# Two output projections that begin inside the last head of their layer

## The chip, the cores and the metric

The kernel runs on one core of one Trainium2 chip. The metric is the device time of one execution in microseconds (us), the median of several runs. TensorE (PE in the rows) multiplies, ScalarE (ACT), VectorE (DVE) and GpSimd (POOL) work on whole tiles, SyncE (SP) issues the loads of the weights.

## The reference

A network of three layers over 512 tokens of width 1024, all in fp32. The change touches the mixers of the first two:

```
# layer 0, MLA: 8 heads of attention, causal softmax
p = softmax(mask(q_h @ k_h^T * scale));  o_h = p @ v_h          # for each head h
m = concat(o_0 .. o_7) @ mla_w_o                                # 1024 x 1024
h = h + rms_norm(m);  h = h + rms_norm(relu(rms_norm(h) @ w1)^2 @ w2)

# layer 1, HGRN2: 8 heads of gated linear recurrence in chunks of 32 tokens
o_h = intra-chunk part (masked k_rel x q_rel) + q_dec @ state   # state chained over 16 chunks
y_h = rms_norm(o_h) * silu(gate_h)
m = concat(y_0 .. y_7) @ hgrn_w_o                               # 1024 x 1024
h = h + rms_norm(m);  then the second MLP
# layer 2: three other mixers and an MLP, not touched
```

Both projections sum over the heads: head k contributes the k-th block of 128 rows of the weight. So a projection can start with the heads that are done, and needs the last head only for its last term.

## The kernel before

The five engines have programs of their own, written out by hand, that meet only through semaphores. Each engine works through its program in order.

**Weights.** All weights are a list of blocks of 128 x 1024 (512 KB). SP loads block b into slot b % 4 of `ring` (L249) when block b - 4 has been used, or, for most blocks, has been split. The right-hand operand is split in the same way (`a_hi`, `a_lo`), and `split_matmul` issues three matmuls for each k, hi x hi, hi x lo and lo x hi (L336 to L338), each 128x128 by 128x512. A tile of output is 8 values of k, thus 24 matmuls, into one PSUM bank. `ring_hi` and `ring_lo` have 4 slots too.

**A projection** of 8 tiles is `gemm_split_pe`: tile u goes to bank u % 4 after its bank is free (`mla_o_free`, `hgrn_o_free`) and its block is split. `to_m_act` squares and copies each finished tile (L561, L562) and then rounds the block four ahead. `to_m_dve` adds up the squares (L574) and then computes that block's rest. Behind the last tile `norm_pe` computes the norm.

**Last heads, MLA.** `mla_pe` goes through the heads. In turn h it projects head h + 1 (`head`, banks 0 to 2), transposes the probabilities of head h (`att_turn_pe`, L516, banks 3 to 5), computes the scores of head h + 1 (L470, banks 0 to 2), and multiplies head h's probabilities by its values (`att_out_pe`, L531, bank 6). ACT takes the exponentials (L491), copies the turned probabilities (`att_turned_act`, L523) and head h's output as `a_hi` (L818). DVE masks the scores (L480), divides (L499 the reciprocal, L506) and computes the low half `a_lo` (`low_y`, L899), which counts `mla_y`. In turn 7 there is no next head. `mla_o` begins behind it.

**Last heads, HGRN.** `hgrn_pe` runs `head(i, nxt, prev)`: the projections of head i + 1 (`project`, 24 matmuls each for q, f, v and g in banks 0 to 3), the norm of head i - 1 (`total`, L417, `spread`, L425, bank 7), and head i itself: pairs (L1314, bank 4), turned keys (L1319, bank 5), chunk states (L1288, banks 5 and 6), output (L1345 and L1350, bank 4). DVE chains the states (L1505), and when the norm is spread computes y and its two halves, which counts `hg_y_split`. ACT writes the turned keys to `kz` (L1416). Heads 1 to 6 are a loop. `head(7, False, True)` has no projections to issue. Behind it come `total(7)`, `spread(7)` and `hgrn_o`. The first four blocks of `hgrn_o` are rounded and split in turn 6, as the next head's blocks would be.

Of the kernel before, what the change touches and what calls it, by code (L numbers as in the profile page):

```python
# [17 lines left out]
NT = D // P  # L18
# [287 lines left out]
def gemm_pe(pe, M, name, tiles, per_tile, rhs, unroll, banks=4, looped=True, first_wait=None):  # L306

    used, free = M.sem("blocks_used"), M.sem(f"{name}_free")

    def tile(i, u):
        pe.wait_ge(free, u + 1 if i is None else i * unroll + (u + 1))
        for blk in range(per_tile):
            b = FIRST[name] + u * per_tile + blk
            wait_block(pe, M, b, i, unroll * per_tile)
            for k in range(BLK):
                kk = blk * BLK + k
                if first_wait and u == 0:
                    first_wait(kk)
                mm = pe.matmul(M.bank(u % banks), block_tile(M, b, k), rhs(kk),  # L320
                               start=(kk == 0), stop=(kk == per_tile * BLK - 1))
            mm.then_inc(used, 1)

    if looped:
        with pe.Fori(0, tiles // unroll) as i:
            for u in range(unroll):
                tile(i, u)
    else:
        for u in range(tiles):
            tile(None, u)  # L330

def split_matmul(pe, M, out, b, k, hi, lo, start, stop):
# [352 lines left out]
def mla_pe(pe, M, R):  # L686
    def total(name, n):
        pe.wait_ge(M.sem("norm_summed"), n + M.past(name, "summed"))
        norm_total_pe(pe, M, M.norm_bank(name), M.ssum).then_inc(M.sem("norm_total"), 1)

    def first_total():
        pe.wait_ge(M.sem("inputs_in"), 16)
        total("norm_0", NT)

    mla_in_pe(pe, M, {(2, 4): first_total, (3, 4): lambda: norm_root_pe(pe, M, "norm_0"),
                      (5, 2): lambda: total("q_lora", 4), (6, 0): lambda: norm_root_pe(pe, M, "q_lora")})

    pe.wait_ge(M.sem("norm_scaled"), 4 + M.past("q_lora", "scaled"))
    pe.wait_ge(M.sem("mla_in_free"), 6)
    for pair in range(4):  # L700
        b, at = FIRST["mla_rope"] + pair // 2, 4 * (pair % 2)
        if pair % 2 == 0:
            wait_block(pe, M, b)
        for k in range(4):
            mm = pe.matmul(M.bank(ROPE_BANK[pair]), block_tile(M, b, at + k), R.proj[:, k, :],
                           start=(k == 0), stop=(k == 3))
        mm.then_inc(M.sem("blocks_used" if pair % 2 else "rope_pairs"), 1)
        if pair == 0:
            total("kv_lora", 2)
        if pair == 1:  # L710
            norm_root_pe(pe, M, "kv_lora")
    pe.wait_ge(M.sem("norm_scaled"), 2 + M.past("kv_lora", "scaled"))

    pe.wait_ge(M.sem("mla_in_free"), 7)

    def head(h):
        b = FIRST["mla_heads"] + h
        wait_block(pe, M, b)
        for k in range(4):
            pe.matmul(M.bank(0), block_tile(M, b, k), R.proj[:, k, :], start=(k == 0), stop=(k == 3))  # L720
        for k in range(2):
            pe.matmul(M.bank(1), block_tile(M, b, 4 + k), R.proj[:, 4 + k, :], start=(k == 0), stop=(k == 1))
        if h == 0:
            pe.wait_ge(M.sem("rope_read"), 2)
        for t in range(QT):
            for k in range(2):
                mm = pe.matmul(M.bank(2)[:, t * P:(t + 1) * P], R.proj[:, 4 + k, t * P:(t + 1) * P],
                               block_tile(M, b, 6 + k), start=(k == 0), stop=(k == 1))
        mm.then_inc(M.sem("blocks_used"), 1)

    def scores(h):
        pe.wait_ge(M.sem("mla_heads_free"), h + 1)
        if h == 0:
            pe.wait_ge(M.sem("rope_turned"), 5)
        half = slice(0, P)
        att_scores_pe(pe, M, "mla", [(R.q[:, h % 2, :], R.k[:, h % 2, :]),
                                     (R.qr[half, h // 2, :], R.krz[:, h % 2, :])])

    head(0)
    scores(0)  # L740
    for h in range(MLA_H):
        if h + 1 < MLA_H:

            pe.wait_ge(M.sem("mla_masked"), h + 1)
            head(h + 1)
        att_turn_pe(pe, M, "mla", R.att, h, 0)
        if h + 1 < MLA_H:
            scores(h + 1)
        if h:
            pe.wait_ge(M.sem("mla_y"), h)  # L750
        att_out_pe(pe, M, "mla", R.att, h, 0, lambda k: R.v[:, h % 2, k * P:(k + 1) * P], 6)
    gemm_split_pe(pe, M, "mla_o", NT, 1, lambda k: M.a_hi[:, k, :], lambda k: M.a_lo[:, k, :], 4,
                  first_wait=lambda k: pe.wait_ge(M.sem("mla_y"), k + 1))
    norm_pe(pe, M, "mla_o", NT + 2)

def mla_act(act, M, R):
# [53 lines left out]
    for h in range(MLA_H):  # L811
        if h + 1 < MLA_H:
            head(h + 1)
        att_turned_act(act, M, "mla", R.att, h, 0)
        if h + 1 < MLA_H:
            att_exp_act(act, M, "mla", R.att, h + 1, 0)
        act.wait_ge(M.sem("mla_out"), h + 1)
        act.activation(M.a_hi[:, h, :], M.bank(6), ACT.Copy).then_inc(M.sem("mla_y_high"), 1)  # L818
        for j in MLA_O_AT.get(h, ()):
            round_block(act, M, FIRST["mla_o"] + j, fresh=True)  # L820
    to_m_act(act, M, "mla_o", 1, 4, 4, round_ahead(act, M))

MLA_O_AT = {5: (0,), 6: (1,), 7: (2, 3)}

def mla_dve(dve, M, R):
# [72 lines left out]

    att_mask_dve(dve, M, "mla", R.att, 0, 0, mask, MLA_SCALE)
    for h in range(MLA_H):
        if h:
            low_y(h - 1)
        att_divide_dve(dve, M, "mla", R.att, h, 0)
        if h + 1 < MLA_H:
            att_mask_dve(dve, M, "mla", R.att, h + 1, 0, mask, MLA_SCALE)
        for j in MLA_O_AT.get(h, ()):
            rest(FIRST["mla_o"] + j)  # L910
# [348 lines left out]
def hgrn_pe(pe, M, R):  # L1259
# [32 lines left out]
    def total(i):  # L1292
        pe.wait_ge(M.sem("hg_squared"), i + 1)
        norm_total_pe(pe, M, M.bank(7), M.sq[:, 0, :]).then_inc(M.sem("hg_total"), 1)

    def spread(i):
        pe.wait_ge(M.sem("hg_inverse"), i + 1)
        norm_spread_pe(pe, M, M.bank(7), lambda c: M.inv[:, c:c + 1].broadcast_to([P, P]))\
            .then_inc(M.sem("hg_spread"), 1)

    def head(i, nxt, prev):
        if nxt:
            project(0, i, 1, (lambda: total(i - 1)) if prev else None)
            project(1, i, 1, (lambda: spread(i - 1)) if prev else None)
        elif prev:
            total(i - 1)
            spread(i - 1)
        pe.wait_ge(M.sem("hg_rel"), i + 1)
        if prev:

            pe.wait_ge(M.sem("hg_y"), i)
        for t in range(QT):
            s = slice(t * P, (t + 1) * P)
            mm = pe.matmul(M.bank(4)[:, s], R.k_rel[:, s], R.q_rel[:, s], start=True, stop=True)  # L1314
        mm.then_inc(M.sem("hg_pairs"), 1)
        pe.wait_ge(M.sem("hg_dec"), i + 1)
        for t in range(QT):
            s = slice(t * P, (t + 1) * P)
            mm = pe.transpose(M.bank(5)[:, s], R.k_dec[:, s], M.t("ident", P))  # L1319
        mm.then_inc(M.sem("hg_keys_turned"), 1)  # L1320
        if nxt:
            project(2, i, 1)
        pe.wait_ge(M.sem("hg_v"), i + 1)
        pe.wait_ge(M.sem("hg_keys_kept"), i + 1)
        states(0, 6)
        states(1, 5)

        def last_states():

            pe.wait_ge(M.sem("hg_chained"), i * 4 + 1)  # L1330
            states(2, 6)
            pe.wait_ge(M.sem("hg_chained"), i * 4 + 2)
            states(3, 5)

        if nxt:
            project(3, i, 1, last_states)
            turn_values(i, 1)
        else:
            last_states()
        pe.wait_ge(M.sem("hg_chained"), i * 4 + 4)  # L1340
        pe.wait_ge(M.sem("hg_pairs_masked"), i + 1)
        for t in range(QT):
            s = slice(t * P, (t + 1) * P)

            pe.matmul(M.bank(4)[:, s], R.v[:, s], R.masked[:, s], start=(t == 0), stop=False,  # L1345
                      skip_group_check=True)
            for r in range(4):
                c = 4 * t + r
                w = slice(c * CH, (c + 1) * CH)
                mm = pe.matmul(M.bank(4)[:, w], R.state[:, c, :], R.q_dec[:, w], start=False, stop=(c == N_CH - 1),  # L1350
                               skip_group_check=True)
        mm.then_inc(M.sem("hg_out"), 1)
# [14 lines left out]
    head(7, False, True)  # L1367
    total(7)
    spread(7)
    pe.wait_ge(M.sem("hg_y_split"), 8)  # L1370
    gemm_split_pe(pe, M, "hgrn_o", NT, 1, lambda k: R.y_hi[:, k, :], lambda k: R.y_lo[:, k, :], 4)
    norm_pe(pe, M, "hgrn_o", NT + 2)

# [1953 lines left out]
```

## Time and profile before

| | us |
|---|---|
| median of 3 runs | 3069.14 (3068.56 to 3069.7) |
| the profiled execution | 3072.35 |
| its span, first to last instruction | 3070.3 |
| TensorE busy | 2849.1 (93%) |
| DVE busy | 1657.3 (54%) |
| ACT busy | 1135.9 (37%) |
| mean granted clock of TensorE | 0.948 of 2.4 GHz |

A row of a timeline gives an instruction, or several of one kind in a row: start, length, engine, line, operation and operands, count, and in brackets the idle time of the engine before it and who ended it. A matmul's length includes its way through the array, so it overlaps the next one's start.

### The profile page before, as it was taken

To read this page: it belongs to the slowest core of one execution; us is meant where nothing else is said; L and a number is where in the kernel's file an instruction comes from. 1 tells how busy PE (TensorE), PEld (TensorE's weight loads), DVE (VectorE), ACT (ScalarE), POOL (GpSimd) and SP (SyncE) were. 2 spreads that over 40 slices of the span, in tenths; PEclk is the share of its full clock that TensorE was granted. 3 is DMA by queue.
4 is the path that set the end of the run, shared out by engine and by line. 5 is a ranking of instruction groups with operands and counts; after the bars stand their busy time and mean duration, and the time that the engine had idled before them with its cause. 6 is when DMAs were issued, how large, how long until landed. Compare 5 with 4: busy or idle time off the path is not lost.

```text
span 3070.3 us, 38355 instructions
## 1 busy us (share of the span) xinstructions
PE 2849.1 (93%) x13679; PEld 2286.6 (74%) x13679; DVE 1657.3 (54%) x2994; ACT 1135.9 (37%) x1860; POOL 116.2 (4%) x108
## 2 busy tenths in 40 slices
PE   7989999989998999998969998989899998999998
PEld 5557888878887788887646886657777776778887
DVE  6225726355554662634874146753687856465462
ACT  4333322235453322223344223852355444232221
POOL 0000000000000000000000000000132210000000
PEclk9989999979997999997989889999999999999999
DMA  3112332312111232322101322002212121333332
GB/s 138 42 48 69 104 97 94 103 41 70 55 55 41 69 110 92 97 92 76 55 1 43 95 65 67 1 15 95 70 62 62 62 62 62 117 99 100 96 96 68
DMA packets 60654, 221.41 MB, mean 72 GB/s; under 512 B 6512, under 2 KB 6640, under 8 KB 60400
## 3 DMA queue, kind: packets, MB, share of 16 engines
q1 hardware_dynamic: 58928, 213.43, 22.3%
q0 software_dynamic: 1600, 6.29, 0.6%
q8 instruction: 80, 1.31, 0.2%
q14 instruction: 46, 0.38, 0.0%
HBM read 215.50 MB, written 4.19 MB: 72 GB/s over the span
## 4 chain that ended last, share of the span: by engine, by line
PE 75%; DVE 11%; issue 5%; ACT 4%; DVEq 3%; DMA 0%; ACTq 0%; POOL 0%; SPq 0%
PE ps L336 21%; PE ps L337 21%; PE ps L338 21%; PE ps L417 1%; DVE work L1792 1%; DVE big L2805 1%; DVEq L2861 1%; DVE ring_lo L286 1%; PE ps L1288 1%; PE ps L425 1%; DVE work L1811 1%; PE ps L1718 1%; PE ps L2155 1%; PE ps L2622 1%; PE ps L1556 1%
## 5 line engine op out<-in xcount | busy, mean ns | idle before, releaser
L336 PE MATMUL ps<-a_hi,ring_hi 128*128 128x512 f32 x1960 | 798.4, 407 | 52.1 <-DVE ring_lo L286 22.7
L286 DVE TENSOR_TENSOR ring_lo<-ring,ring_hi 128x1024 fp32r<-128x1024 f32 x381 | 466.3, 1225 | 603.8 <-ACT ring_hi L279 571.0
L338 PE MATMUL ps<-a_hi,ring_lo 128*128 128x512 f32 x1960 | 776.0, 396 | 0.0
L337 PE MATMUL ps<-a_lo,ring_hi 128*128 128x512 f32 x1896 | 750.2, 396 | 0.0
L279 ACT ACTIVATE ring_hi<-ring 128x1024 fp32r<-128x1024 f32 x381 | 400.5, 1054 | 544.8 <-PE ps L338 541.4
L336 PEld LDWEIGHTS ps<-a_hi,ring_hi 128*128 128x128 f32 x1960 | 376.8, 192 | 141.7 <-issue 26.4
L338 PEld LDWEIGHTS ps<-a_hi,ring_lo 128*128 128x128 f32 x1960 | 375.9, 192 | 81.1
L337 PEld LDWEIGHTS ps<-a_lo,ring_hi 128*128 128x128 f32 x1896 | 364.2, 192 | 81.1 <-issue 7.7
L337 PE MATMUL ps<-hid_lo,ring_hi 128*128 128x512 f32 x960 | 375.4, 391 | 0.0
L336 PE MATMUL ps<-hid_hi,ring_hi 128*128 128x512 f32 x896 | 349.6, 390 | 5.6 <-DVEq L1024 5.6
L338 PE MATMUL ps<-hid_hi,ring_lo 128*128 128x512 f32 x896 | 349.3, 390 | 0.0
L337 PEld LDWEIGHTS ps<-hid_lo,ring_hi 128*128 128x128 f32 x960 | 181.3, 189 | 37.6
L336 PEld LDWEIGHTS ps<-hid_hi,ring_hi 128*128 128x128 f32 x896 | 168.7, 188 | 41.0 <-issue 6.0
L338 PEld LDWEIGHTS ps<-hid_hi,ring_lo 128*128 128x128 f32 x896 | 168.6, 188 | 35.1
L1076 ACT ACTIVATE sq<-ps 128x512 f32<-128x512 f32 x96 | 57.4, 598 | 353.1 <-PE ps L338 301.3
L1094 DVE TENSOR_TENSOR ssum<-sq,ps 128x512 f32<-128x512 f32 x96 | 65.9, 686 | 88.4 <-ACT sq L1076 82.2
L1746 ACT ACTIVATE work<-work 128x128 f32<-128x128 f32 (+3 forms) x128 | 70.0, 551 | 45.0 <-DVE work L1796 45.0
L1682 PE MATMUL ps<-big,work 64*128 64x256 f32 (+3 forms) x384 | 64.9, 481 | 14.0 <-DVE work L1796 8.9
L1023 DVE TENSOR_TENSOR hid_lo<-ssum,hid_hi 128x512 f32 (+1 forms) x96 | 66.4, 692 | 12.4 <-issue 0.9
L1682 PEld LDWEIGHTS ps<-big,work 64*128 64x128 f32 x384 | 46.5, 205 | 32.2 <-issue 18.0
L1096 DVE TENSOR_TENSOR ssum<-ssum 128x512 f32<-128x512 f32 x96 | 66.5, 693 | 7.2
L1792 DVE CUSTOM_DVE_ANT_0 work<-ps,work 128x128 f32<-128x128 f32 (+3 forms) x128 | 54.9, 486 | 24.9 <-issue 24.9
(383 smaller groups left out, 3452.1 us busy)
## 6 DMA issues: line engine op xcount, KB each, us to landing
ring<-weights SPq DMA_DIRECT2D x399, 512.0 KB, 3.5
h<-x SPq DMA_DIRECT2D x1, 2048.0 KB, 9.2
residual<-h POOLq DMA_DIRECT2D x2, 1024.0 KB, 4.8
h<-residual POOLq DMA_DIRECT2D x1, 2048.0 KB, 11.3
out<-h POOLq DMA_DIRECT2D x1, 2048.0 KB, 7.6
tab<-tables SPq DMA_DIRECT2D x1, 1648.0 KB, 15.4
big<-positions SPq DMA_DIRECT2D x1, 256.0 KB, 3.6
col<-columns SPq DMA_DIRECT2D x1, 164.5 KB, 3.9
```

The costliest lines, as they stand in the source:

```text
L279: act.activation(hi, M.ring[:, b % RING, :], ACT.Copy).then_inc(M.sem("blocks_rounded"), 1)
L286: dve.tensor_tensor(lo, M.ring[:, b % RING, :], hi.bitcast(F32), ALU.subtract).then_inc(M.sem("blocks_split"), 1)
L336: pe.matmul(out, w_hi, hi, start=start, stop=False)
L337: pe.matmul(out, w_hi, lo, start=False, stop=False)
L338: return pe.matmul(out, w_lo, hi, start=False, stop=stop)
L1023: dve.tensor_tensor(lo, src, hi.bitcast(F32), ALU.subtract)
L1076: act.activation(M.sq[:, u % 2, :], M.bank(u % 4), ACT.Relu).then_inc(free, 1)
L1094: dve.tensor_tensor(M.ssum[:, :], M.sq[:, u % 2, :], M.norm_bank(norm), ALU.mult)
L1096: dve.tensor_tensor(M.ssum[:, :], M.ssum[:, :], M.ssum[:, :], ALU.mult)
L1682: mm = pe.matmul(M.ps[:, at:at + S_LEN[t]], self.staged[rows, u, t * P:(t + 1) * P], self.kinds[kind][0][rows, 0:S_LEN[t]], start=True, st ...
L1746: e = act.activation(s, s, ACT.Exp, bias=V.ntop[:, x, t:t + 1], scale=1.0, accum_out=V.sum[:, x, t:t + 1])
L1792: dve.tensor_tensor_reduce(V.p[x][:, CAUSAL_AT[t]:CAUSAL_AT[t] + S_LEN[t]], M.ps[:, at:at + S_LEN[t]], m[:, CAUSAL_AT[t]:CAUSAL_AT[t] + S_ ...
```

## The change

Parts of the first tiles of `mla_o` and `hgrn_o` are issued between the steps of the last head, each with the values of k whose heads are done. `part_of_tile_pe` issues such a part. In MLA, these are tiles 0 and 1; ACT and DVE split the four first blocks of `mla_o` one head earlier, ACT puts its rounding between the copies of the turned tiles and the next exponentials, and in the last head DVE computes head 6's low half behind the division of head 7 and no more ahead of it. In HGRN, these are tiles 0 to 3, on TensorE alone.

```diff
+def part_of_tile_pe(pe, M, name, u, y_hi, y_lo, ks):
+    b = FIRST[name] + u
+    wait_split(pe, M, b)
+    for k in ks:
+        mm = split_matmul(pe, M, M.bank(u), b, k, y_hi[:, k, :], y_lo[:, k, :], k == 0, k == NT - 1)
+        if k == NT - 1:
+            mm.then_inc(M.sem("blocks_used"), 1)
...
 # mla_pe
+    part = lambda u, ks: part_of_tile_pe(pe, M, "mla_o", u, M.a_hi, M.a_lo, ks)
...
+        if h + 1 == MLA_H:
+            pe.wait_ge(M.sem("mla_masked"), MLA_H)
+            pe.wait_ge(M.sem("mla_y"), 6)
+            part(0, range(0, 6))
         att_turn_pe(pe, M, "mla", R.att, h, 0)
         if h + 1 < MLA_H:
             scores(h + 1)
         if h:
             pe.wait_ge(M.sem("mla_y"), h)
+        if h + 1 == MLA_H:
+            part(1, range(0, 3))
         att_out_pe(pe, M, "mla", R.att, h, 0, lambda k: R.v[:, h % 2, k * P:(k + 1) * P], 6)
-    gemm_split_pe(pe, M, "mla_o", NT, 1, lambda k: M.a_hi[:, k, :], lambda k: M.a_lo[:, k, :], 4,
-                  first_wait=lambda k: pe.wait_ge(M.sem("mla_y"), k + 1))
+    part(1, range(3, 7))
+    part(0, range(6, 7))
+    pe.wait_ge(M.sem("mla_y"), MLA_H)
+    for u in range(2):
+        part(u, range(7, 8))
+    gemm_split_pe(pe, M, "mla_o", NT, 1, lambda k: M.a_hi[:, k, :], lambda k: M.a_lo[:, k, :], 4, done=2)
...
 # mla_act
         att_turned_act(act, M, "mla", R.att, h, 0)
+        for j in MLA_O_AT.get(h, ()):
+            round_block(act, M, FIRST["mla_o"] + j, fresh=True)
         if h + 1 < MLA_H:
             att_exp_act(act, M, "mla", R.att, h + 1, 0)
         act.wait_ge(M.sem("mla_out"), h + 1)
         act.activation(M.a_hi[:, h, :], M.bank(6), ACT.Copy).then_inc(M.sem("mla_y_high"), 1)
-        for j in MLA_O_AT.get(h, ()):
-            round_block(act, M, FIRST["mla_o"] + j, fresh=True)
...
-MLA_O_AT = {5: (0,), 6: (1,), 7: (2, 3)}
+MLA_O_AT = {4: (0,), 5: (1,), 6: (2, 3)}
...
 # mla_dve
-        if h:
+        if h and h + 1 < MLA_H:
             low_y(h - 1)
         att_divide_dve(dve, M, "mla", R.att, h, 0)
+        if h + 1 == MLA_H:
+            low_y(h - 1)
...
 # hgrn_pe, head(i, nxt, prev)
         elif prev:
+            pe.wait_ge(M.sem("hg_banks_free"), 8)
+            pe.wait_ge(M.sem("hg_y_split"), 6)
+            part(0, range(0, 6))
             total(i - 1)
             spread(i - 1)
+            part(1, range(0, 4))
...
         pe.wait_ge(M.sem("hg_v"), i + 1)
+        if not nxt:
+            part(1, range(4, 6))
+            part(2, range(0, 3))
         pe.wait_ge(M.sem("hg_keys_kept"), i + 1)
         states(0, 6)
         states(1, 5)
+        if not nxt:
+            part(2, range(3, 6))
...
             last_states()
+            pe.wait_ge(M.sem("hg_y_split"), 7)
+            for u in range(3):
+                part(u, range(6, 7))
...
     total(7)
     spread(7)
+    pe.wait_ge(M.sem("hg_gate_free"), 8)
+    part(3, range(0, 7))
     pe.wait_ge(M.sem("hg_y_split"), 8)
-    gemm_split_pe(pe, M, "hgrn_o", NT, 1, lambda k: R.y_hi[:, k, :], lambda k: R.y_lo[:, k, :], 4)
+    for u in range(4):
+        part(u, range(7, 8))
+    gemm_split_pe(pe, M, "hgrn_o", NT, 1, lambda k: R.y_hi[:, k, :], lambda k: R.y_lo[:, k, :], 4, done=4)
```

## Rows read from the trace of the kernel before

**Rows 1.** The page's first part: busy time, share and instructions by engine.

```profile
PE 2849.1 (93%) x13679; PEld 2286.6 (74%) x13679; DVE 1657.3 (54%) x2994; ACT 1135.9 (37%) x1860; POOL 116.2 (4%) x108
```

**Rows 2.** TensorE's timeline around MLA's last head; columns as told above.

```profile
200.88 2.32 PE L531 MATMUL ps<-mla_turned,big 128*128 128x512 f32 x8
210.16 2.40 PE L516 MATMUL ps<-tab,big 128*128 128x128 f32 x10 [6.96 <-DVE big L506]
214.10 4.61 PE L531 MATMUL ps<-mla_turned,big 128*128 128x512 f32 x8 [1.54 <-ACT mla_turned L523]
221.32 0.80 PE L336 MATMUL ps<-a_hi,ring_hi 128*128 128x512 f32 x1 [2.61 <-ACTq L378]
...
226.55 0.39 PE L336 MATMUL ps<-a_hi,ring_hi 128*128 128x512 f32 x1
...
234.76 0.39 PE L336 MATMUL ps<-a_hi,ring_hi 128*128 128x512 f32 x1
```

**Rows 3.** TensorE's timeline, from HGRN's head 6 to tile 4 of `hgrn_o`.

```profile
935.80 0.98 PE L1350 MATMUL ps<-big,m 128*128 128x32 f32 x8
940.93 1.87 PE L417 MATMUL ps<-tab,sq 128*128 128x1 f32 x8 [4.15 <-ACT sq L1425]
...
952.53 5.77 PE L1288 MATMUL ps<-big,m 128*128 128x128 f32 x32 [2.59 <-ACTq L1417]
960.33 0.79 PE L1345 MATMUL ps<-big 128*128 128x128 f32 x2 [2.03 <-DVEq L1508]
...
969.75 1.87 PE L417 MATMUL ps<-tab,sq 128*128 128x1 f32 x8 [0.69 <-ACT sq L1425]
972.09 2.08 PE L425 MATMUL ps<-tab,inv 128*128 128x128 f32 x8 [0.47 <-DVE inv L1514]
977.08 0.79 PE L336 MATMUL ps<-hid_lo,ring_hi 128*128 128x512 f32 x1 [2.91 <-DVEq L1024]
...
1000.73 0.39 PE L336 MATMUL ps<-hid_lo,ring_hi 128*128 128x512 f32 x1
```

**Rows 4.** ACT's timeline, MLA's heads 6 and 7.

```profile
196.49 1.36 ACT L523 ACTIVATE mla_turned<-ps 128x512 f32<-128x512 f32 x3
...
203.10 0.40 ACT L491 ACTIVATE big<-big,mla_turned 128x128 f32<-128x128 f32 x1 [5.25 <-DVE mla_turned L483]
...
205.20 0.19 ACT L491 ACTIVATION_READ_ACCUMULATOR big<-big,mla_turned 128x1 f32 x1
```

**Rows 5.** DVE's timeline, the reciprocal of MLA's head 7.

```profile
208.59 0.17 DVE L499 RECIPROCAL mla_turned<-mla_turned 128x4 f32<-128x4 f32 x1
```

**Rows 6.** SP's timeline: six loads of weights, the first at 194.81.

```profile
194.81 38.51 SPq L249 DMA_DIRECT2D ring<-weights  x6
```

**Rows 7.** The loads' line over the same stretch: from issue to landing.

```profile
DMA to landing us min/median/max: 3.5/3.6/4.4
```

**Rows 8.** TensorE's timeline in the loop of HGRN's heads.

```profile
899.87 0.48 PE L336 MATMUL ps<-a_hi,ring_hi 128*128 128x512 f32 x1
...
904.18 1.05 PE L417 MATMUL ps<-tab,sq 128*128 128x1 f32 x8 [1.30 <-ACT sq L1425]
905.09 0.49 PE L336 MATMUL ps<-a_hi,ring_hi 128*128 128x512 f32 x1
```

**Rows 9.** DVE's timeline: HGRN's last head, then the tiles of `hgrn_o`.

```profile
943.03 0.18 DVE L1514 RECIPROCAL inv<-root 128x4 f32<-128x4 f32 x1
...
953.71 3.35 DVE L1505 SCALAR_TENSOR_TENSOR m<-m,big,ps 128x128 f32<-128x128 f32 x8 [2.84 <-PE ps L1288]
...
986.67 1.23 DVE L286 TENSOR_TENSOR ring_lo<-ring,ring_hi 128x1024 fp32r<-128x1024 f32 x1 [0.74 <-ACT ring_hi L279]
```

**Rows 10.** ACT's timeline: the first tile of `hgrn_o` is squared.

```profile
984.61 0.60 ACT L561 ACTIVATE sq<-ps 128x512 f32<-128x512 f32 x1 [12.78 <-PE ps L338]
```

**Rows 11.** Windows: length, busy PE, PEld, DVE, ACT, POOL, clock, DMA share, GB/s.

```profile
860.00:900.00 40.00, 38.70 (x246) 34.35 (x245) 24.61 (x42) 23.51 (x32) 0.00 (x0) 1.00 0.22 66
900.00:911.00 11.00, 9.70 (x40) 7.64 (x40) 4.61 (x8) 6.91 (x10) 0.00 (x0) 0.84 0.16 48
```

More of the change, by code:

```diff
@@ L1299, in spread @@
             .then_inc(M.sem("hg_spread"), 1)
+    part = lambda u, ks: part_of_tile_pe(pe, M, "hgrn_o", u, R.y_hi, R.y_lo, ks)
     def head(i, nxt, prev):
```

## The prediction

> **What bounds the kernel now.** I read the page first: TensorE is busy for 93% of the span [rows 1], so the kernel runs at TensorE's pace, and only time in which TensorE waits or runs at its low clock can be won. Then I read the two places that the diff touches in TensorE's timeline, and for each the timelines of ACT and DVE, to see what ended each wait.
>
> First place, the last head of the MLA layer [rows 2]. The output matmuls of head 6 begin at 200.88 and end at about 203.1. Nothing is left to project (there is no head 8), so TensorE sits idle for 6.96 us, until the softmax of head 7 is divided. Then come the transposes (2.40 us), the output (4.61 us), another wait, and at 221.32 the output projection. The reader should see two losses there: the idle time, and matmuls at half speed behind it. From 221.32 to 226.55 twelve matmuls take 0.436 us each, which is the 1.2 GHz level; from 226.55 to 234.76 thirty-six take 0.228 us each, the 2.4 GHz level. Tile 2 of the projection begins at 234.76, so from the end of head 6 to there it is 31.65 us.
>
> Second place, the last head of HGRN [rows 3]: free at about 936.6, and tile 4 of its projection begins at 1000.73, 64.1 us later. The norm's total takes 1.87 us there and 1.05 in the loop [rows 3, 8]: the low level again.
>
> **The change, part by part.** No matmul is added or removed: 48 of `mla_o` (tiles 0 and 1, three matmuls for each of 8 k) and 96 of `hgrn_o` (tiles 0 to 3) are issued in other places, and each tile's stay in their order.
>
> *First layer.* Work between 203.1 and tile 2 if all is at 2.4 GHz: 48 matmuls x 0.228 = 10.9; transposes, half of 2.40 = 1.2; output 2.3, as head 6's at 200.88 [rows 2]; the first matmul after a change of kind costs about 0.1 more (see the second layer), twice: 0.2. Sum 14.6. Does anything wait? Fill 1 (18 matmuls) lasts 203.1 to 207.2. The probabilities: the exponentials of head 7 end at 205.4 [rows 4]; today DVE then does a weight remainder and a low half first, and its reciprocal starts only at 208.59, 1.57 before the transposes at 210.16 [rows 2, 5]. With `low_y` moved behind, and the block's remainder done a head earlier, the reciprocal starts at about 205.45 and the transposes can start at 207.0, under fill 1. The wait `mla_y` >= 7 now includes a low half put behind the division (about 0.7 after 207.0), still before the transposes end at 208.4. Fill 2 (9 matmuls, 2.1) covers ACT's 1.36 us of copies [rows 4]. Fill 3 (15 matmuls, 3.4) covers head 7's copy and low half (0.6 + 0.7 and hand-overs). No idle time is left: 31.65 - 14.6 = **17.0 us won**.
>
> *What is moved on ACT, DVE and SP.* ACT now rounds a block (about 1.0 us) after its copies of the turned tiles and before the next exponentials. At the last of these, two blocks are behind the copies that end at 197.85 [rows 4], so they end at about 199.9, if block 20 is in; ACT then waits for DVE's mask until 203.1 anyway (5.25 us of idle time today [rows 4]), so 3.2 us are left over. Block 20's load is issued at 194.81 [rows 6] and a load lands 3.5 to 4.4 us later [rows 7], so at 199.2 at worst. DVE's two remainders (twice 1.23 [rows 9]) follow its mask at 203.0 and end at 205.4, just as the exponentials end: cost 0, at most 0.2. Loads of blocks 22 to 24 get earlier on SP's queue, which waits for the splits; nobody waits for them. In HGRN nothing moves on those engines.
>
> *Second layer.* I take fixed costs from a head in the loop. From 899.87 (end of one head's output) to 936.6 it is 36.7 us [rows 3, 8], with 96 matmuls (21.9), one wait of 1.30, the low clock's 1.76 (below) and some nine changes of kind. A total of norms takes 0.91 there, from its start to that of the matmul behind it, which itself takes 0.49 where 0.39 is usual: 0.1 per change of kind [rows 3, 8]. So total, spread, pairs, turned keys, states and output take 36.7 - 21.9 - 1.3 - 1.8 - 0.8 = 10.9, of which the turned values (absent in the last head) take 0.4. The second total and spread add 0.9 + 0.9 (half of 2.08, overlapping). Fixed work 12.3; matmuls 96 x 0.228 = 21.9; five changes 0.5. Waits that stay:
> - before the first total, squares at 940.93; fill 1 ends at 940.7: 0.2.
> - total to spread: the total ends at 941.8, but DVE's reciprocal starts at 943.03, behind a remainder [rows 9]; spread at 943.3: 1.4. Nothing was put here.
> - Fills 2 to 4 (12, 15 and 9 matmuls) then bring the states to about 951.5, against 952.53 now. DVE's chain, at 953.71 today, starts at 952.6; 6.6 us pass from its start to the output at 960.33 [rows 3, 9], so the output starts at 959.3. PE ends its fill (9 more) at 959.0: 0.4.
> - square before the last total 0.7, reciprocal before the last spread 0.5 [rows 3], both with nothing to fill them.
> - After the spread, 21 matmuls cover DVE's 2.9 us and 12 more end the tiles, at about 974.4. Tile 4 then needs block 4's split: ACT's square starts at 984.61 and DVE's remainder at 986.67 takes 1.23 [rows 9, 10], so 3.3 us from the end of tile 0 to its slot. After the change tile 0 ends only 2 us before tile 3, so TensorE waits about **1.6**. This is what is late next.
>
> Waits 4.8. Sum 12.3 + 21.9 + 0.5 + 4.8 = 39.5, so 24.6 are won if the clock stays high throughout.
>
> **The clock** has no row for the new order, so I bound it. In the loop the same mixture runs at 1.00 for 40 us at a time, but after a wait of 1.30 us and a total the clock falls once: 0.84 over 11 us, 1.76 us lost [rows 8, 11]. The last head will have four such short waits. None of them falling costs 0; all of them 4 x 1.7 = 7. I take one to two, 2.5 us, since one of the two loop stretches shows none. Second layer: **22.1 won**.
>
> Total 17.0 + 22.1 = 39.1. The profiled execution took 3072.35 us (span 3070.3), 3.2 above the median of the runs; it would take 3033.3, and the median 3069.14 - 39.1 = **3030.0 us**. Behind both projections TensorE runs without a pause up to the norm, which depends on the last tile alone, so the gain passes on whole.
>
> **Rivals.**
> - *The clock often falls in HGRN's last head.* All at the low level it would take 96 x 0.43 + 2 x 12.3 + 1.6 = 67.5, so 3.4 lost instead of 24.6 won. For it: its end is entirely low today. Against: it is so behind waits of 2 to 4 us, which the fills close. Half of the way gives 10.6; total 27.6: 3041.5.
> - *The gain is not passed on*, because weights come late: 3069. Against: loads land within 4.4 us and are issued when a slot is free [rows 7].
> - *One layer's fills come too late*: for instance ACT's rounding waits for block 20 and holds up the exponentials of head 7. It decides from a landing after 202, 7 us behind the issue, and each us beyond costs one; if the whole first gain is lost: 3047.
> - *Slower: the low level spreads.* The fills hop between banks 0 to 3 and 4 to 7; if this kept TensorE at 1.2 GHz, the first layer would take 48 x 0.43 + 2.4 + 4.6 = 27.6 (4.0 won), the second loses 3.4, and every matmul of the 240 behind them that is still slow costs 0.2 us. It is slower by over 0.2% from some 33 of those; with all, 3069.1 - 0.6 + 48 = 3117. Against: the loop's heads hop among all eight banks at 1.00 [rows 11]. The Trainium skill (TensorE: Matmul & The Clock Gate, "A second HAM failure mode: psum-queue depth-cycling") says that cycling through PSUM banks makes TensorE pause between groups and the clock swing between its levels. By that rule this rival would win; the trace of the loop disagrees with it.
>
> **How the numbers follow.** Forecast (one to two falls; with none 3027.5, with four 3034.5): 0.80. Often low: 0.11. Fills late: 0.03. Not passed on: 0.03. Low level spreads: 0.03. Falls elsewhere in the program may shift with the start times, 1.7 us each, one or two either way. Range: 3027.5 less two such falls, 3024, to the middle of the second case, 3041; 0.15 is left out. A measurement of this kernel can't tell 0.2% (6 us) from no change: faster 0.94, same 0.03, slower 0.03.
>
> **What would show it.** In the changed profile: no idle time of TensorE between 203 and 217, transposes near 207.2, tile 2 of `mla_o` near 217.7, the clock 1.00 there; HGRN's output, 8.7 us from 960.33 to the squares before the last total, taking 4.4; a wait of 1 to 2 us for DVE's remainder before tile 4; tile 4 some 22 us nearer to the start of the last head than now. I am wrong if the clock is below 0.85 over the last head, if the transposes of head 7 start after 208.5, or if the stages behind got longer.

## The result, and the profile after

The changed kernel takes 3031.35 us, the median of 4 runs (3027.25 to 3036.69), against 3068.85 before (3068.19 to 3069.7): ratio 0.9879, 95% interval 0.9862 to 0.9896, so 37.5 us or 1.2% faster. The forecast was 3030.0, with 3024 to 3041. The profiled execution is the slowest of the four: 3036.69 us, span 3034.7. The new lines shift the line numbers: the split matmuls are L346 to L348 now, `att_turn_pe` L526, `att_out_pe` L541, `total` L427, `spread` L435, the states L1311, the output L1382 and L1387.

The page's first part, to be set against [rows 1]:

```profile
PE 2835.3 (93%) x13679; PEld 2274.5 (75%) x13679; DVE 1656.1 (55%) x2994; ACT 1135.9 (37%) x1860; POOL 116.4 (4%) x108
```

The same 13679 matmuls keep TensorE busy for 13.8 us less. Nothing was taken out, so this part of the gain is clock; the rest of it is idle time.

TensorE's timeline around MLA's last head, the rows that answer to [rows 2]:

```profile
203.49 2.32 PE L541 MATMUL ps<-mla_turned,big 128*128 128x512 f32 x8
205.73 0.50 PE L346 MATMUL ps<-a_hi,ring_hi 128*128 128x512 f32 x1
...
209.99 1.25 PE L526 MATMUL ps<-tab,big 128*128 128x128 f32 x10
211.00 0.48 PE L346 MATMUL ps<-a_hi,ring_hi 128*128 128x512 f32 x1
...
213.17 2.32 PE L541 MATMUL ps<-mla_turned,big 128*128 128x512 f32 x8
215.24 0.48 PE L346 MATMUL ps<-a_hi,ring_hi 128*128 128x512 f32 x1
...
220.11 0.39 PE L346 MATMUL ps<-a_hi,ring_hi 128*128 128x512 f32 x1
```

No row has an idle time in brackets. From the start of head 6's output to tile 2 (the row at 220.11) it is 16.62 us, where [rows 2] have 33.88 (200.88 to 234.76): 17.26 won. The transposes take 1.25 instead of 2.40, at the high level of the clock, and the first matmul behind them 0.48, where the first one of `mla_o` in [rows 2] took 0.80 at the low level.

Windows from the end of head 6's output in HGRN to tile 4 of `hgrn_o`, first of before, then of after (length, busy PE, PEld, DVE, ACT, POOL, clock, DMA share, GB/s):

```profile
936.60:1000.70 64.10, 49.06 (x214) 42.96 (x214) 23.62 (x43) 14.98 (x24) 0.00 (x0) 0.73 0.08 26
```

```profile
921.60:966.00 44.40, 40.64 (x214) 34.83 (x213) 19.81 (x40) 12.31 (x21) 0.00 (x0) 0.88 0.04 13
```

64.1 became 44.4: 19.7 won. Idle time fell from 15.0 to 3.8 us and TensorE's busy time from 49.1 to 40.6, with the clock up from 0.73 to 0.88. The waits that are left, in TensorE's timeline of the changed kernel:

```profile
928.14 2.08 PE L435 MATMUL ps<-tab,inv 128*128 128x128 f32 x8 [1.14 <-DVE inv L1555]
...
951.51 1.46 PE L427 MATMUL ps<-tab,sq 128*128 128x1 f32 x8 [0.69 <-ACT sq L1466]
953.44 2.07 PE L435 MATMUL ps<-tab,inv 128*128 128x128 f32 x8 [0.48 <-DVE inv L1555]
955.17 0.77 PE L346 MATMUL ps<-hid_lo,ring_hi 128*128 128x512 f32 x1
...
966.05 0.47 PE L346 MATMUL ps<-hid_lo,ring_hi 128*128 128x512 f32 x1 [1.44 <-DVE ring_lo L286]
```

These are the waits that the prediction left standing, the new one for DVE's remainder of block 4 (1.44) among them. Both spreads run at the low level: 2.08 and 2.07 us for what takes 1.05 at the high one. The window around the last spread shows how much of the low clock lies there, (1 - 0.60) x 8.5 = 3.4 us by the granted clock. By the rows it is 3.0 us of work (the total, the spread and nine matmuls, each against its length at the high level); the rest is a low clock during waits, which costs nothing:

```profile
951.50:960.00 8.50, 8.02 (x30) 6.94 (x31) 3.22 (x6) 0.17 (x1) 0.00 (x0) 0.60 0.01 2
```

### The profile page after: what moved, and what is told of

Read it like the earlier page. It is cut to its first block, busy times and chain, and to the rows that moved or that the text cites. A ratio compares the mean times of both kernels' runs of the same rounds, so it can differ in the third digit from the quotient of the medians.

```text
span 3034.7 us, 38355 instructions
## 1 busy us (share of the span) xinstructions
PE 2835.3 (93%) x13679; PEld 2274.5 (75%) x13679; DVE 1656.1 (55%) x2994; ACT 1135.9 (37%) x1860; POOL 116.4 (4%) x108
## 4 chain that ended last, share of the span: by engine, by line
PE 78%; DVE 10%; ACT 4%; issue 3%; DVEq 3%; ACTq 0%; DMA 0%; POOL 0%; SPq 0%
PE ps L346 21%; PE ps L348 21%; PE ps L347 21%; PE ps L427 1%; DVE work L1833 1%; PE ps L480 1%; DVE big L2846 1%; DVEq L2902 1%; DVE ring_lo L286 1%; PE ps L731 1%; PE ps L1311 1%; DVE work L1852 1%; PE ps L435 1%; PE ps L1759 1%; PE ps L2196 1%
## 5 line engine op out<-in xcount | busy, mean ns | idle before, releaser
L346 PE MATMUL ps<-a_hi,ring_hi 128*128 128x512 f32 x1960 | 797.9, 407 | 49.5 <-DVE ring_lo L286 22.8
L348 PE MATMUL ps<-a_hi,ring_lo 128*128 128x512 f32 x1960 | 774.8, 395 | 0.0
L346 PEld LDWEIGHTS ps<-a_hi,ring_hi 128*128 128x128 f32 x1960 | 375.9, 192 | 138.4 <-issue 26.3
L348 PEld LDWEIGHTS ps<-a_hi,ring_lo 128*128 128x128 f32 x1960 | 375.6, 192 | 80.9
L346 PE MATMUL ps<-hid_hi,ring_hi 128*128 128x512 f32 x896 | 349.6, 390 | 5.5 <-DVEq L1047 5.5
L348 PE MATMUL ps<-hid_hi,ring_lo 128*128 128x512 f32 x896 | 349.3, 390 | 0.0
L347 PEld LDWEIGHTS ps<-hid_lo,ring_hi 128*128 128x128 f32 x960 | 181.6, 189 | 37.5
L346 PEld LDWEIGHTS ps<-hid_hi,ring_hi 128*128 128x128 f32 x896 | 168.7, 188 | 40.9 <-issue 5.9
L348 PEld LDWEIGHTS ps<-hid_hi,ring_lo 128*128 128x128 f32 x896 | 168.6, 188 | 35.1
```

The costliest lines, as they stand in the source:

```text
L346: pe.matmul(out, w_hi, hi, start=start, stop=False)
L347: pe.matmul(out, w_hi, lo, start=False, stop=False)
L348: return pe.matmul(out, w_lo, hi, start=False, stop=stop)
```

## The experiments

Each kernel is the changed kernel with one edit, unless told otherwise. "Before" is the kernel before, run on the same chip. In the table: the median of the runs, and where it tells more, a stretch of the profile. Stretch A is from the start of head 6's output to tile 2 of `mla_o`, stretch B from the end of head 6's output (the first matmul of `hgrn_o`) to tile 4 of `hgrn_o`.

| run | median us (range) | before | stretch |
|---|---|---|---|
| changed | 3031.35 (3027.3 to 3036.7) | 3068.85 | A 16.62, B 44.4 |
| e1 first layer only | 3051.48 (3050.8 to 3055.2) | 3069.68 | A 16.60 |
| e2 second layer only | 3050.27 (3048.6 to 3053.2) | 3069.68 | B 44.5 |
| e3 splits late | 3039.76 (3037.5 to 3041.4) | 3069.68 | A 20.36, B 44.5 |
| e4 low half first | 3033.54 (3030.3 to 3037.7) | 3069.68 | A 17.41, B 43.0 |
| e5 middle wait filled | 3033.27 (3030.7 to 3034.6) | 3070.80 | B 42.0 |
| e6 tile 0 first | 3032.22 (3029.1 to 3033.4) | 3070.80 | B 43.1 |
| e7 all waits filled | 3026.93 (3025.0 to 3029.6) | 3070.80 | B 37.7 |
| e8 changed, again | 3034.84 (3028.9 to 3036.9) | 3070.80 | A 16.58, B 44.5 |
| e9 total later in the loop | 3017.86 (3015.3 to 3025.2) | 3068.51 | B 43.1 |
| e10 e7 and e9 | 3013.86 (3011.4 to 3016.2) | 3068.51 | B 37.7 |

**e1 and e2: each half alone.** All hunks of the diff in `hgrn_pe` are taken back in e1, all others in e2 (with `MLA_O_AT` as before).

> The first layer's half of the change alone; HGRN's last head and projection are as before. My sum says 31.65 us between the end of head 6's output and tile 2 of mla_o become 14.4 to 14.6: 17.2 won, so 3051.7 us. If instead the first layer gains only because of where the clock's falls happen to lie, or if part of the gain comes from the second layer starting elsewhere, the time is off that by more than 3 us: under 3048 or over 3055. If the first fills came too late it would stay at 3060 or more.

> The second layer's half alone; MLA's engines are all as before. Theory: 24.6 won at the high clock throughout, less 1.7 for each fall of the clock in the last head. The changed kernel's trace shows 10.2 us at the low level there and 19.8 won, so 3049 us, between 3044.5 (no fall) and 3051. Rival, the clock often low in that head: the median is over 3053. If the halves don't depend on each other, the two gains add up to 37 to 39, the whole change's.

The first half gives 18.2 us by the medians (ratio 0.9939, 0.9926 to 0.9953), the second 19.4 (0.9935, 0.9921 to 0.9948). Both lie where they were expected (3051.48 for 3051.7, 3050.27 for 3049). Together they give 37.6, and the whole change gave 37.5 in its own runs and 36.0 in those of e8, so within the spread of the runs the halves add up, and each is about the size that its own stretch shows (17.3 and 19.6).

**e3: the first four blocks of `mla_o` split in their old places.**

```diff
-        for j in MLA_O_AT.get(h, ()):
-            round_block(act, M, FIRST["mla_o"] + j, fresh=True)
         if h + 1 < MLA_H:
             att_exp_act(act, M, "mla", R.att, h + 1, 0)
         act.wait_ge(M.sem("mla_out"), h + 1)
         act.activation(M.a_hi[:, h, :], M.bank(6), ACT.Copy).then_inc(M.sem("mla_y_high"), 1)
+        for j in MLA_O_AT.get(h, ()):
+            round_block(act, M, FIRST["mla_o"] + j, fresh=True)
...
-MLA_O_AT = {4: (0,), 5: (1,), 6: (2, 3)}
+MLA_O_AT = {5: (0,), 6: (1,), 7: (2, 3)}
```

> The whole change, but ACT rounds and DVE splits the first four blocks of mla_o in the places of before. Theory: the moved splits cost nothing where they are and are needed there. Late, DVE's remainder of block 18 waits for ACT until after the exponentials of head 7, the reciprocal starts 2.5 us later, and TensorE waits some 2.4 us before the transposes; DVE's low half of head 7 comes behind the remainders of blocks 19 and 20, some 1.4 us after fill 3 ends. In all 3.8 us slower than the whole change: tile 2 of mla_o begins 18.2 us after the end of head 6's output, against 14.4. Rival: the fills cover it, and it stays at 14.4 to 15.

TensorE's timeline of e3:

```profile
212.63 1.31 PE L526 MATMUL ps<-tab,big 128*128 128x128 f32 x10 [2.09 <-DVE big L516]
...
222.80 0.50 PE L346 MATMUL ps<-a_hi,ring_hi 128*128 128x512 f32 x1 [1.20 <-DVE a_lo L920]
```

and DVE's:

```profile
209.91 1.23 DVE L286 TENSOR_TENSOR ring_lo<-ring,ring_hi 128x1024 fp32r<-128x1024 f32 x1 [3.79 <-ACT ring_hi L279]
211.05 0.17 DVE L509 RECIPROCAL mla_turned<-mla_turned 128x4 f32<-128x4 f32 x1
```

Both waits came where they were expected: 2.09 (expected 2.4) and 1.20 (1.4). The stretch is 3.74 longer (3.8). DVE's rows show why: it waits 3.79 us for ACT's rounding of a block, with the division of head 7 queued behind that block's remainder. So the moved splits carry 3.7 us of the first layer's gain, though they touch no matmul. The medians are 8.4 us apart, but by the runs' spread (e8) they can't size this; the profiled executions of e3 and of the changed kernel, both at a mean clock of 0.954, have spans 3.8 apart (3038.5 and 3034.7).

**e4: the low half ahead of the division again.**

```diff
-        if h and h + 1 < MLA_H:
+        if h:
             low_y(h - 1)
         att_divide_dve(dve, M, "mla", R.att, h, 0)
-        if h + 1 == MLA_H:
-            low_y(h - 1)
```

> The whole change, but in the last head DVE computes head 6's low half ahead of the division, as before. Theory: it waits for ACT's copy, so the reciprocal starts 1.05 us later and the transposes 1.57 behind it; fill 1 covers all but 0.7 us. Tile 2 of mla_o begins 15.1 us after the end of head 6's output, against 14.4. Rival: fill 1 covers all of it, 14.4. The whole time can't tell 0.7 us; the trace can.

```profile
207.47 1.31 PE L526 MATMUL ps<-tab,big 128*128 128x128 f32 x10 [0.60 <-DVE big L516]
```

TensorE waits 0.60 before the transposes and the stretch is 0.79 longer (expected 0.7); the median can't tell this. How narrow the margin is shows in the last row of the division in the changed kernel:

```profile
208.29 1.27 DVE L516 TENSOR_SCALAR big<-big,mla_turned 128x128 f32<-128x128 f32 x4
```

It ends at 209.56, and the transposes start behind fill 1 at 209.99: the probabilities are ready 0.43 us early.

**e5: the middle wait filled.** Six of the twelve matmuls move.

```diff
             total(i - 1)
+            part(1, range(0, 2))
             spread(i - 1)
-            part(1, range(0, 4))
+            part(1, range(2, 4))
```

> The whole change, and six matmuls of tile 1 of hgrn_o move from behind head 6's spread to between its total and its spread, where TensorE waits 1.1 to 1.4 us for DVE's reciprocal. Theory: the wait goes, 1.1 us, and with it the fall of the clock behind it, another 1.7: 2.8 us less between head 6's output and tile 4 than the 44.4 of the changed kernel. Rival: the clock falls because of the thin matmuls of the total, whatever stands between: only about 1.1 less.

Windows over stretch B of e5:

```profile
918.80:960.80 42.00, 39.02 (x214) 33.27 (x214) 19.88 (x40) 12.36 (x21) 0.00 (x0) 0.92 0.04 13
```

and TensorE's timeline:

```profile
925.56 1.06 PE L435 MATMUL ps<-tab,inv 128*128 128x128 f32 x8
...
928.32 1.13 PE L1344 MATMUL ps<-big 128*128 128x128 f32 x8 [0.31 <-DVE pair L1561]
```

The stretch is 2.4 shorter (expected 2.8, the rival 1.1). Idle time fell by 0.8 only, since a new wait of 0.31 for y came up; TensorE's busy time fell by 1.6, one fall of the clock. The spread takes 1.06 now. The total with its thin matmuls stands there as before, so it is not they alone that made the clock fall. The median on that chip is 1.6 below e8's, within the runs' spread. The length of one stretch would not settle it either, for without any edit in the last head it was 44.4 to 44.5 in four profiles but 43.0 in e4 and 43.1 in e9. What settles it is the place: in all seven profiles that have this wait of 1.14 (changed, e2, e3, e4, e6, e8, e9) the clock falls right behind it, and in the three where it is filled (e5, e7, e10) it doesn't.

**e6: tile 0 ends earlier.**

```diff
-    part(3, range(0, 7))
+    part(3, range(0, 5))
     pe.wait_ge(M.sem("hg_y_split"), 8)
-    for u in range(4):
+    for u in range(3):
         part(u, range(7, 8))
+    part(3, range(5, 8))
```

> The whole change, and behind the last spread only 15 matmuls of tile 3 come before the last terms of tiles 0 to 2; the other 9 of tile 3 come behind them. Theory: tile 0 ends 1.4 us earlier, so ACT's and DVE's split of block 4 is ready when TensorE is, and the wait before tile 4 (1.6 by my sum) goes: 1.4 to 1.6 less. Rival: the wait before tile 4 is not for that split, or the clock falls in place of it: no less.

```profile
920.10:963.20 43.10, 40.64 (x215) 34.70 (x214) 19.82 (x40) 12.30 (x21) 0.00 (x0) 0.88 0.04 13
```

The wait before tile 4 is gone, the stretch 1.3 shorter (expected 1.4 to 1.6), busy time and clock as in the changed kernel. So that wait was for the split of block 4, released by the end of tile 0.

**e7: all waits filled.**

```diff
-    total(7)
-    spread(7)
     pe.wait_ge(M.sem("hg_gate_free"), 8)
-    part(3, range(0, 7))
+    part(3, range(0, 1))
+    total(7)
+    part(3, range(1, 2))
+    spread(7)
+    part(3, range(2, 6))
     pe.wait_ge(M.sem("hg_y_split"), 8)
-    for u in range(4):
+    for u in range(3):
         part(u, range(7, 8))
+    part(3, range(6, 8))
```

with the edit of e5.

> Both of the two edits before, and one k of tile 3 each in the waits before the last total and before the last spread. Theory: four waits filled, 1.1 + 1.6 + 0.7 + 0.5 less 0.9 by which the last total and spread now start later and block 4's split with them: 3.0 less, and with most of the falls of the clock in that head gone up to 5 more; 3023 to 3028 us. Rival, thin matmuls make the clock fall whatever stands between: 3 less, 3028 to 3029.

```profile
918.80:956.50 37.70, 36.45 (x214) 30.49 (x214) 19.83 (x40) 12.33 (x21) 0.00 (x0) 1.00 0.05 15
```

The clock is 1.00 over the whole stretch, and the stretch is 6.7 shorter than in the changed kernel: 2.5 of idle time, 4.2 of busy time. The median, 3026.93, is 7.9 below e8's on the same chip, and their ranges overlap by 0.7 us only (3025.0 to 3029.6 against 3028.9 to 3036.9). The rival, 3028 to 3029 with the falls where they were, is ruled out by the clock, not by the median; e10 has the same last head, again with 37.7 and 1.00.

**e8: the changed kernel again.**

> The changed kernel once more, beside the three variants on the same chip. Theory: the runs of the changed kernel spread over some 9 us because the clock's falls lie elsewhere from run to run, each 1.7 us; the median is again 3030 to 3033, and a second profile shows falls in other places of the program with the same order of instructions. Rival: the spread came from one chip, and here the runs lie within 2 us.

The median, 3034.84, is above the 3030 to 3033 that were expected. Again the runs spread, over 7.9 us, so the rival of a single odd chip is out. The page of this execution and of the first profile differ by 7.8 us in span (3026.9 and 3034.7) and by 8.1 in TensorE's busy time, for the same matmuls in the same order:

```profile
PE 2827.2 (93%) x13679; PEld 2268.9 (75%) x13679; DVE 1656.1 (55%) x2994; ACT 1135.4 (38%) x1860; POOL 116.2 (4%) x108
```

One of the places lies in MLA's first heads, which the change doesn't touch. The windows of the first profile, then of e8:

```profile
90.00:105.00 15.00, 12.77 (x46) 6.99 (x45) 3.40 (x15) 3.14 (x10) 0.00 (x0) 0.89 0.00 0
```

```profile
90.00:105.00 15.00, 12.18 (x53) 7.35 (x52) 3.40 (x15) 5.13 (x14) 0.00 (x0) 1.00 0.11 33
```

Both have the same wait of 2.23 us ahead of the matmuls there; behind it the clock fell in one execution and held in the other. What decides this was not settled.

**e9 and e10: the same wait in the loop.** In e9 the total of the previous head's norm is issued two k later:

```diff
-    def project(j, i, ahead, between=None):
+    def project(j, i, ahead, between=None, at=4):
...
-            if k == 4 and between:
+            if k == at and between:
                 between()
...
-            project(0, i, 1, (lambda: total(i - 1)) if prev else None)
+            project(0, i, 1, (lambda: total(i - 1)) if prev else None, 6)
```

> The whole change, and in the loop of HGRN's heads the norm's total is issued behind 18 matmuls of the next head's first projection instead of 12. TensorE waits 1.30 us there today in each of heads 1 to 6, and the clock fell behind some of these waits (five falls between 670 and 900 us in the changed kernel's profile, 1.7 us each). Theory, the short wait is what lets the clock fall: 6 x 1.3 = 7.8 for the waits and up to 5 x 1.7 = 8.5 for the falls, 16 us less: 3015 to 3018. Rival, the falls come from the thin matmuls of total and output whatever stands between: 8 less, 3023 to 3025. Second rival, the later total makes the norm and its y late, and the loop gains nothing.

> The edit of the run before on top of all waits filled. Theory: both gains add, 16 + 5 to 8 below the changed kernel: 3008 to 3013 us, with no fall of the clock between 700 and 980 us. Rival, falls only move to other places: 3016 or more.

Windows over the loop (in e9 with the first 5 us of the last head), of the changed kernel, then of e9:

```profile
700.00:910.00 210.00, 202.18 (x1161) 175.27 (x1160) 118.64 (x209) 111.84 (x150) 0.00 (x0) 0.97 0.19 56
```

```profile
700.00:910.00 210.00, 210.00 (x1247) 183.29 (x1246) 129.43 (x230) 119.74 (x161) 0.00 (x0) 1.00 0.20 63
```

TensorE, idle for 7.8 of 210 us before, has no idle time left, and the clock went from 0.97 to 1.00. The thin matmuls are the same. The totals of three heads in a row of the changed kernel, then of two in e9, show what a turn costs:

```profile
745.42 1.05 PE L427 MATMUL ps<-tab,sq 128*128 128x1 f32 x8 [1.31 <-ACT sq L1466]
782.18 1.05 PE L427 MATMUL ps<-tab,sq 128*128 128x1 f32 x8 [1.30 <-ACT sq L1466]
817.33 1.05 PE L427 MATMUL ps<-tab,sq 128*128 128x1 f32 x8 [1.30 <-ACT sq L1466]
```

```profile
808.01 1.05 PE L427 MATMUL ps<-tab,sq 128*128 128x1 f32 x8
841.80 1.05 PE L427 MATMUL ps<-tab,sq 128*128 128x1 f32 x8
```

A turn lasts 36.76 us with a fall of the clock behind the wait, 35.15 without one, and 33.79 in e9: a fall costs 1.61 and the wait 1.36. In the ten profiles that have these six waits the clock falls behind three or four of them; in e9 and e10 it falls behind none. Of the five falls that the expectation counted in the changed kernel, the one at 672 lies behind another wait, of 3.10 us, ahead of the loop, and e9 and e10 still have it. So the rows give 6 x 1.36 + 4 x 1.61 = 14.6.

e9 takes 3017.86 us (ratio 0.9843, 0.9829 to 0.9857), 13.5 below the changed kernel's first runs and 17.0 below e8's (16 expected, 8 by the rival). Over the whole program TensorE's busy time in e9, 2826.9, is 8.4 below the first profile's but level with e8's 2827.2, for falls lie elsewhere each time: the clock's share is shown in the loop, and the medians can't size it. e10 takes 3013.86 us (0.9824, 0.9810 to 0.9838), 54.7 us or 1.8% below the kernel before, the best of all; that is 0.9 above the expected 3008 to 3013 and under the rival's 3016. The clock doesn't fall between 700 us and the end of `hgrn_o`; in the norm behind it, at 969, it does, before the 980 up to which the expectation had none:

```profile
700.00:900.00 200.00, 200.00 (x1188) 174.77 (x1187) 122.36 (x218) 112.47 (x150) 0.00 (x0) 1.00 0.19 60
900.00:965.00 65.00, 63.67 (x356) 53.85 (x356) 36.32 (x60) 27.35 (x42) 0.00 (x0) 1.00 0.24 73
```

Its gain over e9 is 4.0 by the medians and 5.4 by stretch B (43.1 to 37.7), since e9's last head happened to lose less to the clock than the changed kernel's.

## Why the prediction was right, point by point

- **What bounds the kernel.** Right: time came from TensorE's waits and its low clock in two places. In the first layer idle time gave 11.1 us (6.96 + 1.54 + 2.61 in [rows 2], none now) and the clock 6.2; in the second, idle time 11.3 and the clock 8.4. Two fifths of the gain are clock.
- **First layer, 17.0 won.** Measured 17.26. The transposes start 6.5 us after the output's start (the sum had 6.3), right behind fill 1, with 0.43 us to spare. e3 shows that the splits had to move; that they cost nothing where they are now shows in e1, where head 6's output starts at 200.87, as in the kernel before.
- **Second layer at the high clock, 39.5.** The stretch of 44.4 less the 4.7 that the low clock cost (next point) is 39.7. That it is so near is in part luck: two errors offset each other. The waits were 0.1 + 1.14 + 0.24 + 0.69 + 0.48 + 1.44 = 4.1, for 4.8 in the sum, each in its place; the work was 35.6 for 34.7. "This is what is late next", the split of block 4, was right; e6 took it away.
- **The clock, 2.5 us.** This is the term that was mis-sized: by the rows the matmuls at the low level took 4.7 us longer than at the high one, 1.7 behind the middle wait and 3.0 around the last spread, nearly twice the 2.5. e7, with the clock at 1.00, agrees: 4.2 less busy time. The prediction counted one or two falls; it was three falls' worth at the loop's 1.6, two of them in a row around the last spread. Its bound of 7 held. So the second layer gave 19.7 for 22.1: 2.2 more for the clock, 0.9 more work, 0.7 less waiting.
- **Passed on whole.** By the two stretches, 17.3 + 19.7 = 37.0; by the medians 37.5, and 36.0 beside e8. Nothing was lost behind: from tile 4 of `hgrn_o` to the end it is 2069.6 us before and 2068.6 after. The profiled spans differ by 35.6 only, since this execution was 2.6 us late already when stretch A began (203.49 for 200.88). The first median lies only 1.4 from the forecast, which is luck within the spread: the same kernel had 3034.84 in e8.
- **The signs of being wrong.** One came up by its letter: the transposes start at 209.99, after 208.5. It was given as a time on the old trace, and the whole stretch stands 2.6 later; counted from the start of head 6's output they start at 6.5, where the sign means 7.6. The clock over the last head, 0.88, was above 0.85. Tile 4 came 19.7 nearer, for 22, which is the clock's term again.
- **The rivals.** Clock often low in HGRN's last head: no, 0.88, and 19.7 won where its half-way case has 10.6. Fills too late: e3 makes a like case, for 3.7 us, and the changed kernel doesn't have it. Not passed on: no. Low level spreads because the banks are changed so often: no. e7 issues its fills in still smaller groups, and has 1.00 over its last head. The Trainium skill (TensorE: Matmul & The Clock Gate, "A second HAM failure mode: psum-queue depth-cycling") puts the clock's swings down to brief idle times of TensorE between groups of matmuls, and these to the cycling through banks. For the cycling this case's traces disagree (1.00 in e7); for the idle times they agree: e5, e7 and e9 filled short waits, and the falls behind them went.
- **The margin of the measurement.** The falls elsewhere were taken as one or two either way, thus up to 6.8 us from lowest to highest. The changed kernel's runs spread over 9.4 and 7.9 us, so that was somewhat too little. The kernel before ran within 1.5 us in its first runs and within 9.4 in those beside e9.

## What to carry to other kernels

Where an engine waits at the end of a chain of dependent steps, look for a sum that already has most of its terms, and issue those in the wait, before moving anything else; then check what is released later in bulk (here the banks and splits of the next tiles). Count a short wait of TensorE not by its own length alone: here waits of 0.5 to 1.4 us cost about as much again in clock (3.8 and 4.7 us in the last head), and filling them with matmuls that are needed anyway gave more than the wait showed. And look for the same wait in the loop first, where it is paid in every turn.

## What was unexpected of the hardware

- The clock falls behind short waits, but not behind each. The wait of 1.30 us, ahead of a total's thin matmuls (0.84 over 11 us in [rows 11]), had a fall behind it three or four times out of six, the wait of 1.14 us in the last head seven times out of seven. With the wait filled and the same thin matmuls in place, the clock held for 210 us (e9) and over a whole last head (e7). What decides between fall and no fall behind the same wait is open.
- The same program, with its instructions in the same order, differs by 8 us from one execution to another, all of it in TensorE's busy time. For changes of a few us in such a kernel, the median of four runs doesn't decide; the stretch in the trace tells more, read by its waits and by where the clock falls, since its length moves by a fall too.
